# A two-block fp32 network kernel: where the split of the next weights, the head norms, the clears and the retention scores stand in the attention rounds

## The reference, cut to what matters

```python
def second_block(x, ...):
    h = rms_norm(x, norm_mix)
    na_q, na_k, na_v, r_q, r_k, r_v, r_g = split(h @ w_in)      # 3 x 512, 256, 256, 512, 512 columns
    na_out = neighbourhood_attention(na_q, na_k, na_v, rpb)     # 8 heads of 64; 8 rows x 64 columns of tokens;
        # per block of 16 columns: softmax(q k^T / 8 + bias, masked to a window of 16 of 32 columns) v
    rq, rk = rotary(r_q), rotary(r_k) / 8                       # 4 heads of 64, values of 128
    ret = retention(rq, rk, r_v, fwd) + flip(retention(flip ..., bwd))
        # chunks of 128: (q k^T * decay) v inside a chunk, q * state across chunks
    ret = (ret - mean) * rsqrt(var + eps) * gain                # per head
    x = x + concat(na_out, silu(r_g) * ret) @ w_out
    x = x + square(relu(rms_norm(x) @ w_up)) @ w_down
    return rms_norm(x)
```

## Time and profile before

| | us |
|---|---|
| median of 3 runs (lowest, highest) | 1880.41 (1879.92, 1880.64) |
| the profiled execution's own time | 1880.53 |
| its span, first to last instruction | 1878.5 |
| TensorE matmul busy | 1835.7 (98%) |
| VectorE busy | 970.2 (52%) |
| ScalarE busy | 621.5 (33%) |
| GpSimd busy | 31.8 (2%) |

### The profile page before, as it was taken

The page is one execution under the profiler, slowest core; times in us unless marked ns, Lnnn a source line. Parts: engine busy times, 40 slices in busy tenths (PEclk is TensorE's granted clock), DMA queues, the critical chain, the costliest instruction groups (busy, mean ns, idle before and its releaser), DMA issues.

```text
span 1878.5 us, 20299 instructions
## 1 busy us (share of the span) xinstructions
PE 1835.7 (98%) x8338; PEld 1510.0 (80%) x8338; DVE 970.2 (52%) x1291; ACT 621.5 (33%) x889; POOL 31.8 (2%) x34
## 2 busy tenths in 40 slices
PE   8999999999999999999999999999988899999998
PEld 6888888878888888888888888888766788888887
DVE  6434434637765435455543443465655564545354
ACT  6222222444332223333421322255434442222233
POOL 0000000000000000000000000001111000000000
PEclk9999999999999999999999999999988999999999
DMA  4332322322123322232232332244211223233322
GB/s 170 101 97 94 97 94 93 111 90 79 57 90 101 101 90 96 96 100 95 96 101 90 101 101 90 87 132 134 75 40 35 78 90 101 91 101 100 100 91 68
DMA packets 52811, 176.37 MB, mean 94 GB/s; under 512 B 6336, under 2 KB 9024, under 8 KB 52720
## 3 DMA queue, kind: packets, MB, share of 16 engines
q1 hardware_dynamic: 51520, 172.51, 28.7%
q0 software_dynamic: 448, 1.24, 0.2%
q10 hardware_dynamic: 752, 1.33, 0.2%
HBM read 170.86 MB, written 2.10 MB: 92 GB/s over the span
## 4 chain that ended last, share of the span: by engine, by line
PE 92%; DVE 4%; ACT 2%; issue 1%; DMA 0%; SPq 0%; DVEq 0%
PE ps L1328 28%; PE ps L1330 28%; PE ps L1329 28%; PE ps L1348 2%; PE ps L1349 1%; PE ps L1350 1%; DVE wl L731 1%; PE ps L1609 1%; DVE tm L1156 1%; PE ps L1620 0%; ACT wh L362 0%; PE ps L1484 0%; PE ps L1634 0%; PE ps L1358 0%; PE ps L1487 0%
## 5 line engine op out<-in xcount | busy, mean ns | idle before, releaser
L1328 PE MATMUL ps<-Hhi,wh 128*128 128x512 f32 x1544 | 612.1, 396 | 6.5 <-DVE Hlo L736 6.5
L1329 PE MATMUL ps<-Hlo,wh 128*128 128x512 f32 x1544 | 604.2, 391 | 0.0
L1330 PE MATMUL ps<-Hhi,wl 128*128 128x512 f32 x1544 | 603.8, 391 | 0.0
L731 DVE TENSOR_TENSOR wl<-raw,wh 128x1024 fp32r<-128x1024 f32 (+1 forms) x320 | 387.7, 1212 | 133.3 <-ACT wh L362 131.5
L362 ACT ACTIVATE wh<-raw 128x1024 fp32r<-128x1024 f32 (+1 forms) x320 | 332.3, 1039 | 318.7 <-PE ps L1330 298.8
L1328 PEld LDWEIGHTS ps<-Hhi,wh 128*128 128x128 f32 x1544 | 292.1, 189 | 74.8 <-issue 12.1
L1329 PEld LDWEIGHTS ps<-Hlo,wh 128*128 128x128 f32 x1544 | 292.1, 189 | 62.2 <-issue 2.2
L1330 PEld LDWEIGHTS ps<-Hhi,wl 128*128 128x128 f32 x1544 | 291.7, 189 | 61.3
L1328 PE MATMUL ps<-Ahi,wh 128*128 128x512 f32 x792 | 308.2, 389 | 0.3 <-DVE Alo L1185 0.3
L1330 PE MATMUL ps<-Ahi,wl 128*128 128x512 f32 x792 | 308.1, 389 | 0.0
L1329 PE MATMUL ps<-Alo,wh 128*128 128x512 f32 x792 | 308.1, 389 | 0.0
(11 more groups left out here) (258 smaller groups left out, 1196.5 us busy)
## 6 DMA issues: line engine op xcount, KB each, us to landing
raw<-in_w_gu SPq DMA_DIRECT2D x87, 512.0 KB, 3.3
raw<-in_w_d SPq DMA_DIRECT2D x32, 512.0 KB, 3.5
raw<-in_w_up SPq DMA_DIRECT2D x32, 512.0 KB, 3.3
raw<-in_w_dn SPq DMA_DIRECT2D x32, 512.0 KB, 3.5
raw<-in_w_d SPq DMA_DIRECT2D x16, 384.0 KB, 3.1
raw<-in_w_v SPq DMA_DIRECT2D x8, 512.0 KB, 3.5
raw<-in_w_cc SPq DMA_DIRECT2D x8, 512.0 KB, 3.3
raw<-in_w_cu SPq DMA_DIRECT2D x8, 512.0 KB, 3.4
```

Source lines behind the costliest of these rows:

```text
L731: dve.tensor_tensor(WL[u % 3][:, 0:n], RAW[u % 3][:, 0:n], f32(WH[u % 3][:, 0:n]), ALU.subtract).then_inc(s["wl"], 1)
L1328: pe.matmul(ps, wh[:, c], hi[:, k, :], start=(k == 0), stop=False)
L1329: pe.matmul(ps, wh[:, c], lo[:, k, :], start=False, stop=False)
L1330: last = pe.matmul(ps, wl[:, c], hi[:, k, :], start=False, stop=(k == nb - 1))
```

## The change

Six edits, all in the 16 rounds above and at the start of `out2`:

1. From n = 6 on, `hi` and `lo` are called for unit n+3 instead of n+2, and later in the round: `hi(n+3)` behind the copy of `na_t(p)`, `lo(n+3)` behind the unit's result and ahead of `na_s(p+2)`. `hi(n+2)`, `lo(n+2)` at the start stay for n up to 6; the first output unit has none.
2. `ret_mean` stands ahead of `na_x`, `ret_y` of head h in rounds 8, 9, 11, 12, ScalarE's `rows` in rounds 7, 9, 11, 12.
3. The zero chunks of all four heads are cleared by GpSimd, one memset each for both chunks, with a semaphore `rz`.
4. `ret_s(1)` moves from round 7 into round 5; the decay products of heads 2 and 3 move from round 8 to 6, into tiles and banks of their own; the states of head 3 are made ahead of head 2's; `ret_n(1)` moves from unit 7 to 8.
5. VectorE's `na_o` stands a round later and ahead of `na_x`.
6. The gate: ScalarE's Silu stands ahead of the copy of `na_t(p)`, `rg_out` is cut in two, the second part (`rg_lo`) behind `lo(n+3)`.

```diff
@@ retention tiles and banks
-    RT_S, RT_Q, RT_G = [1, 0, 0, 2], [2, 1, 1, 0], [2, 1, 0, 2]
-    RB_S, RB_O, RB_KV = [5, 4, 2, 6], [2, 7, 2, 7], [2, 6, 5, 6]
+    RET_S = [SS2[:, :], SS[:, :], RS2[:, :], RS3[:, :]]
+    RT_Q, RT_G = [2, 1, 2, 0], [1, 2, 0, 1]
+    RB_S, RB_O, RB_KV = [5, 4, 5, 4], [2, 7, 2, 7], [2, 6, 6, 5]
@@ pool_program, behind the subtraction of the means
+        for h in range(4):
+            if h == 2:
+                pool.wait_ge(s["rot"], 4)
+            pool.memset(SFB[h][:, 0:4:3, :], 0.0).then_inc(s["rz"], 1)
+
         pool.wait_ge(s["nam"], 16)
-        pool.wait_ge(s["rot"], 4)
@@ act_program, the loop over n
-            hi(u + 2)
+            if n <= 6:
+                hi(u + 2)
...
             if n == 6:
                 ret_o(0)
                 ret_o(1)
-                ret_kv(2)
-                ret_kv(3)
-            if n in (7, 9, 10, 11):
-                rows(7 + (7, 9, 10, 11).index(n), TA[6], TA[7], TA[8])
+            if n in (7, 9, 11, 12):
+                rows(7 + (7, 9, 11, 12).index(n), TA[6], TA[7], TA[8])
             if n in (9, 10):
                 ret_o(n - 7)
+            if n > 12:
+                rg_silu(n - 13)
             if 7 <= n < 15:
                 na_t(p)
-                if n in (9, 11, 13):
-                    na_o((n - 9) // 2)
+            if n >= 6:
+                hi(u + 3)
+            if 7 <= n < 15:
                 na_t(p + 1)
+            if n in (9, 11, 13, 15):
+                na_o((n - 9) // 2)
+            if n == 6:
+                ret_kv(3)
+                ret_kv(2)
+            if n > 12:
+                rg_out(n - 13)
             if 6 <= n < 14:
                 na_e(p + 2)
-            if n == 15:
-                na_o(3)
-            if n > 12:
-                rg_silu(n - 13)
-                rg_out(n - 13)
@@ dve_program, ret_kv
-            own.add(dve.memset(SFB[h][0:64, 0, :], 0.0))
-            own.add(dve.memset(SFB[h][64:P, 3, :], 0.0))
-            dve.wait_ge(s["rkc"], 2 * h + 2)
+            dve.wait_ge(s["rz"], h + 1)
+            dve.wait_ge(s["rkc"], 2 * (0, 1, 3, 2)[h] + 2)
@@ dve_program, the loop over n
-            lo(u + 2)
-            if 7 <= n < 15:
-                na_x(p)
+            if n <= 6:
+                lo(u + 2)
...
             if n == 6:
+                ret_s(2)
+                ret_s(3)
                 ret_q(3)
             if n == 7:
+                ret_mean(0)
+                ret_kv(3)
+            if n == 9:
+                ret_mean(1)
+            if n in (10, 12, 14):
+                na_o((n - 10) // 2)
+            if 7 <= n < 15:
+                na_x(p)
+            if n == 7:
                 ret_kv(2)
-                ret_kv(3)
-                ret_mean(0)
-            if n == 8:
-                ret_s(2)
-                ret_s(3)
-            if 9 <= n < 13:
-                ret_y(n - 9)
-                if n < 12:
-                    ret_mean(n - 8)
+            if n in (8, 9, 11, 12):
+                ret_y((8, 9, 11, 12).index(n))
+            if n in (10, 11):
+                ret_mean(n - 8)
             if n == 15:
                 na_o(3)
... (the unit's result out of PSUM)
-            if n in (9, 11, 13):
-                na_o((n - 9) // 2)
+            if n > 12:
+                rg_out(n - 13)
+            if n >= 6:
+                lo(u + 3)
+            if n > 12:
+                rg_lo(n - 13)
             if 6 <= n < 14:
                 na_s(p + 2)
-            if n > 12:
-                rg_out(n - 13)
         rg_out(3)
+        rg_lo(3)
@@ act_program and dve_program, out2
-            hi(u + 2)      # and lo(u + 2)
+            if n > 0:
+                hi(u + 2)  # and lo(u + 2)
@@ pe_program
     ret_kv(1): waits for rsd 4 (was 1); heads in the order 3, 2
     ret_s(1): waits for rsd 2 (was nm 7 and rst 4)
     ret_o(h), h > 1: waits for nm 5 + h (was nm 8, for h = 3 alone)
     na_s(0): waits for rsd 4 (was 2);  na_o(0): for rst 4 (was rsd 4)
-            if n == 7:
+            if n == 8:
                 ret_n(1)
...
             if n == 5:
                 ret_o(0)
+                ret_s(1)
...
                 na_t(p)
-                if n == 7:
-                    ret_s(1)
-                else:
+                if n > 7:
                     na_o(p - 2)
                     na_o(p - 1)
```

More of the change, by code:

```diff
@@ L234, in build @@
            for h, o in enumerate((oAhi + 4 * KB, oAhi + 6 * KB, oAlo + 4 * KB, oAlo + 6 * KB))]
+    RS2, _ = sb("RS2", [P, T], off=oAlo)
+    RS3, _ = sb("RS3", [P, T], off=oAlo + 2 * KB)
     PT2, _ = sb("PT2", [P, T], off=oAhi + 6 * KB)
@@ L601, in ret_kv @@
             kv = four(BK[RB_KV[h]][:, :])
-            act.wait_ge(s["rkv"], h + 1)
+            act.wait_ge(s["rkv"], (1, 2, 4, 3)[h])
             act.activation(SFB[h][0:64, 1, :], kv[0:64, 0, :], ACT.Copy).then_inc(s["rkc"], 1)
@@ L1136, in ret_s @@
             dve.wait_ge(s["rsc"], h // 2 + 1)
-            dve.tensor_tensor(four(RT[RT_S[h]]), four(BK[RB_S[h]][:, :]),
+            dve.tensor_tensor(four(RET_S[h]), four(BK[RB_S[h]][:, :]),
                               DG[:, h, :].unsqueeze(1).broadcast_to([P, 4, P]), ALU.mult).then_inc(s["rsd"], 1)
@@ L1182, in rg_out, with rg_lo @@
                                      op0=ALU.mult, op1=ALU.mult).then_inc(s["rgo"], 1)
+        def rg_lo(i):
             dve.wait_ge(s["rgo"], i + 1)
             dve.wait_ge(s["rah"], i + 1)
-            dve.tensor_tensor(Alo[:, 4 + i, :], g, f32(Ahi[:, 4 + i, :]), ALU.subtract).then_inc(s["ral"], 1)
+            dve.tensor_tensor(Alo[:, 4 + i, :], RT[RT_G[i]], f32(Ahi[:, 4 + i, :]),
+                              ALU.subtract).then_inc(s["ral"], 1)
         dve.wait_ge(s["dg"], 1)
@@ L1557, in ret_kv @@
             else:
-                pe.wait_ge(s["rsd"], 1)
+                pe.wait_ge(s["rsd"], 4)
                 pe.wait_ge(s["rst"], 2)
-            for h in (2 * hp, 2 * hp + 1):
+            for h in ((0, 1), (3, 2))[hp]:
                 for c in range(4):
@@ L1568, in ret_s @@
             if hp == 1:
-                pe.wait_ge(s["nm"], 7)
-                pe.wait_ge(s["rst"], 4)
+                pe.wait_ge(s["rsd"], 2)
             for c in range(4):
@@ L1579, in ret_o @@
             b = RB_O[h]
-            pe.wait_ge(s["rst"], h + 1)
+            pe.wait_ge(s["rst"], (1, 2, 4, 3)[h])
             pe.wait_ge(s["rq"], h + 1)
@@ L1584, in ret_o @@
                 pe.wait_ge(s["rkd"], 8)
-            if h == 3:
-                pe.wait_ge(s["nm"], 8)
+            if h > 1:
+                pe.wait_ge(s["nm"], 5 + h)
             for c in range(4):
                 tc = slice(c * P, c * P + P)
-                pe.matmul(BK[b][:, tc], RV[:, c, h * P:h * P + P], RT[RT_S[h]][:, tc], start=True, stop=False)
+                pe.matmul(BK[b][:, tc], RV[:, c, h * P:h * P + P], RET_S[h][:, tc], start=True, stop=False)
                 p = pe.matmul(BK[b][:, tc], SFB[h][:, c, :], QFB[h][:, tc], start=False, stop=True)
@@ L1601, in na_s @@
             if p == 0:
-                pe.wait_ge(s["rsd"], 2)
+                pe.wait_ge(s["rsd"], 4)
             else:
@@ L1628, in na_o @@
             if p == 0:
-                pe.wait_ge(s["rsd"], 4)
+                pe.wait_ge(s["rst"], 4)
             elif cb == 0:
```

5 lines of the change are left out of this document (3 added, 2 removed).

## The result

The changed kernel takes 1848.51 us (median of 4 runs, 1847.41 to 1849.09) against 1880.51 (1879.92 to 1880.64) of the kernel before in the same comparison: 32.0 us less, a ratio of 0.983 [0.9813, 0.9847]. Forecast were 1846.0, in a range of 1842 to 1854. The profiled execution took 1849.09 us with a span of 1847.3.

A forecast was written before the change was run, and what follows sets the result against it. TensorE was taken to be held up by transposes waiting for ScalarE copies and VectorE scaling, and by the clock falling behind long waits. 21.1 us of waits plus 13.4 of clock, 34.5, off 1880.5 gave 1846.0 us, range 1842 to 1854.

The forecast's parts named there:

- What bounds the kernel: Rounds at 1330 to 1480 us: TensorE waits 27.0 us, mainly transposes waiting for ScalarE copies or VectorE scaling; clock falls behind.
- The split at the end of the unit: L362 and L731 (1.04 and 1.23 us) leave the scores-to-scaled-tile chain; VectorE starts next scores 0.1 to 0.2 us late, free.
- Unit 5 and the clears: Before the first retention product: the 1.3 us wait becomes 0.45; clears on GpSimd were taken to cost nothing.
- Rounds 7 to 12 and 14: Round lengths of 9.1, 9.55, 10.7, 11.5, 9.5, 9.1 and, for round 14, 8.5 us.
- Round 13: First Silu with its 1.28 us table load stands ahead of the copy: a wait of 0.9, length 9.75 us.
- Output unit: First output unit starts 2.5 us late, last block waits 0.5; 8.4 us from unit 15's end, against 5.99.
- Rival 1: The 2.5 us wait ahead of the output unit brings the clock down: 2 to 3 us, 1848.5; chance 0.17.
- Table loads: Two more ScalarE loads of 1.28 us, one hidden, the other making 0.4 us of round 14's waits; no drain counted.
- Rival 3: Many small waits in the rounds keep the clock low, slower than before: 1920 if all nine rounds; chance 0.03.
- The sum: Whole kernel: 21.1 us of waits and 13.4 of clock go, 34.5 us in all, giving 1846.0.
- The two terms of the sum: Waits fall from 27.3 to 6.2, 21.1 us; clock gives 13.4 us, from five slow stretches behind waits over 2 us.
- The signs of being wrong: Mechanism wrong if transposes (L1620) keep waits above 2 us; size wrong if rounds 12 to 14 take over 10 each.

The follow-up runs named there:

- nosplit: Changed kernel with the split of the next weights back at the start of each round, all other edits kept: 1859.15 us.
- pool: Changed kernel with GpSimd's bias additions held until TensorE's scores of that round are done: 1847.26 us.
- afterwl2: silu with GpSimd's additions held until VectorE's split of that round is over, instead of TensorE's scores: 1840.98 us.
- silu: both with the gate's Silu put behind the exponentials and copies, so ScalarE changes tables once: 1841.36 us.
- twice2: Changed kernel with each GpSimd bias addition of rounds 8 and later done twice, same result: 1847.68 us.
- tail: Changed kernel with ScalarE's last attention output copy ahead of the split of unit 18: 1844.91 us.
- splitnorm: Kernel before with the split's and the norms' moves together, retention scores, clears, Silu and attention output copies as before: 1858.58 us.
- both: Changed kernel with the edits of tail and of pool together: 1843.78 us.
- splitonly: Kernel before with only the split of the next weights moved to the end of each unit from round 6 on: 1866.57 us.
- oldnorm: Changed kernel with the head norms back in their old order, split and all else as changed: 1861.46 us.
- oldclear: Changed kernel with the clears of the state tiles back on VectorE: 1850.1 us.
- normonly: Kernel before with only the head norms moved (means ahead of the scaling, multiplications and ScalarE's steps in later rounds): 1866.88 us.

## Why the prediction was right, and what it missed

- **What bounds the kernel**: right. 27.0 us of waits fell to 6.7 (forecast 6.2, of which 0.5 did not show), and slices 30 and 31 went back to nine tenths. The kernels with one move alone show that split and norms were both in the chain: 13.4 and 13.0 us alone, 21.3 together, not 26.4. In rounds 9 and 11 either move takes away much of the same waits (round 9: 4.2 and 5.1 us alone, 6.5 together; round 11: 3.4, 5.9 and 6.4); in round 12 it is the other way, the norms' move alone costs 2.7 us there and with the split moved it costs nothing.
- **The split at the end of the unit**: right. No transpose waits for it, and without it (nosplit) five wait up to 3.3 us. Its free ride ended where the prediction did not look: at GpSimd.
- **Unit 5 and the clears**: wait of 0.45 forecast, 0.35 measured; the clears cost nothing and their way off VectorE gives 1.6 us.
- **Rounds 7 to 12 and 14**: within 0.31 us each. Waits in them were forecast one by one, and the largest error is round 14, 8.5 against 8.19.
- **Round 13**: the step that failed. I had VectorE 1.7 us late into it and one wait of 0.9 for a copy. There are two, 0.89 for the scaling and 1.24 for the copy. I took VectorE's durations from rows in which GpSimd was idle beside it; the new order puts the norm's product and the split where GpSimd adds the bias. Of the way from 11.17 to 8.78 us, pool and afterwl2, which took that away, gave back 0.6 and 0.5, silu 1.3. The forecast had priced the Silu at a wait of 0.9.
- **Output unit**: wait of 2.5 forecast, 2.42 measured, for the reason given. The unit itself was forecast at full clock and ran at 0.76. From the end of unit 15 to its end it took 9.81 us instead of 8.4: the term missed by 1.4. In the trace of twice2, where the clock did not fall behind the same wait, it took 8.5. Rival 1, with a chance of 0.17, was right on this piece, and its price (2 to 3 us) was too high, for the clock cost 1.3 to 1.5. That its total of 1848.5 is the time measured is luck: half of the miss is round 13, of which it says nothing.
- **Table loads**: two more, as forecast (ScalarE has 891 instructions against 889), and no idle time beside them: the load at 1419.14 lasts 1.28 us and the Silu starts at 1420.44. By the Trainium skill (ScalarE: Activation LUTs, What ACT_TABLE_LOAD costs) some 1380 ns of drain would have come on top; this trace does not agree.
- **Rival 3** (many small waits keep the clock low): did not happen. Rounds with waits of 0.5 to 1.24 us stand at full clock, 1.00 from 1351.50 to 1440.00 in tail. The rule of the Trainium skill named there did not act on waits mostly some 9 us apart, nor on the 0.89 and 1.24 of round 13; the two close ones of splitnorm, which cost 1.4 us of clock, are the nearest thing to it in these runs.
- **The sum**: 34.5 forecast, 32.0 measured. From round 7 to the end of the first output unit the trace is 2.8 us above the forecast: round 13 and the output unit account for 1.4 each, rounds 8, 11 and 12 for 0.6 together, and 0.3 came back in rounds 7 and 14 each. The profiled execution reaches round 7 at 1352.48, where tail, pool, both, silu, twice2 and afterwl2, which have the same order up to there, stand at 1351.57 to 1352.18 and the forecast at 1351.7, so 0.3 to 0.9 us of its length is this execution's, not the change's.
- **The two terms of the sum**: of the waits 20.6 us went (27.3 to 6.7), where 21.1 were forecast. The two spans differ by 31.2 us, so 10.6 are left for the clock, where 13.4 were taken. 1.5 of the 2.8 between them is the clock of the output unit and 0.8 is round 7's start at 1352.48 instead of 1351.7; no run here places the rest. The prediction speaks of five waits of over 2 us; there are six in five stretches, since the one of 2.06 ahead of L1574 ends 2.7 us behind the one of 3.04.
- **The signs of being wrong**: no transpose waits over 2 us, and of rounds 12 to 14 one takes over 10 us (11.17), not each.

What stays open: when the clock falls. Single waits of up to 1.35 us left it at 1.00 in every trace. One of 1.89 us (splitonly, round 11) brought it down. One of 2.27 us did in oldnorm and did not in splitonly, one of 2.42 or 2.43 did in six traces (changed kernel, pool, oldnorm, oldclear, nosplit, normonly) and did not in twice2. In splitnorm and splitonly 1.16 us was enough, 2.1 us behind one of 0.51. So the length of a wait does not decide it by itself, and no run here shows what else does. The share of the retention scores' move in round 7 was not run by itself.

## What to carry to other kernels

In an in-order queue, work that nobody needs soon (the split of weights a unit ahead) belongs where the bottleneck engine does its short products, and behind every piece that someone waits for; look at the last round too, where the loop's order meets the next stage. Two moves out of one chain don't add up: here the second gave 8 us where it gave 13 by itself, and in one round the first made things worse until the second came. When a VectorE instruction is moved, look at what GpSimd does at that moment before its duration is taken from the old trace.

## What the runs showed of the hardware

- VectorE instructions with both inputs in SBUF and GpSimd additions hold each other up when they overlap: the norm's product 0.69 to 1.74 us, the split 1.23 to 2.27, GpSimd's pair of additions 2.56 to 3.53. Both the product that starts 0.08 us behind an addition and the split that starts 0.10 behind one grow by 1.05 us, most of the addition's 1.29. Additions with one input in PSUM and row maxima stay at 680 and 686 ns on average in twice2, where GpSimd works beside them. The Trainium skill (SBUF — State Buffer, Who interferes with whom) has the rule: a lock on a shared pair of ports, taken by two SBUF inputs and not by one outside certain modes. The trace agrees, also in that the scalings, which it counts among the instructions that can take the pair, grew from 354 ns to as much as 1.39 us.
- TensorE's clock fell behind a single wait of 2.42 us in the changed kernel (mean 0.76 over the next 7.21 us) and stayed at 1.00 behind the same wait in twice2; waits of 2.27 us went both ways too (1.00 in splitonly, 0.63 over 4.66 us in oldnorm). The shortest single wait with a fall behind it is 1.89 us (splitonly: 0.65 over 4.62 us), the longest without one in all traces is that 2.42. Waits up to 1.35 us left it at 1.00 when they stood alone, but 1.16 us close behind 0.51 (splitnorm) was followed by 3 us of slow products.
